# A crossed running product in a chunked RWKV inverse, and sixteen modulation units moved to the gated linear mixer

## The chip, the cores and the metric

One core of a Trainium2 chip runs the whole program. The metric is the device time in microseconds; the median of three runs of the kernel before is 2090.2 us (2086.09 to 2093.96).

## The reference, cut to what matters

The program computes two transformer blocks and a mixture of experts on 512 tokens of width 1024. Two parts of it matter here. The RWKV mixer of the first block is a recurrence over tokens with 8 heads of 64:

```python
def step(S, inp):
    r_t, w_t, k_t, v_t, a_t, b_t = inp
    sa = jnp.einsum("bhij,bhj->bhi", S, a_t)
    S = S * w_t[:, :, None, :] + sa[..., None] * b_t[:, :, None, :] + v_t[..., None] * k_t[:, :, None, :]
    return S, jnp.einsum("bhij,bhj->bhi", S, r_t)
```

The second block's gated linear mixer (`gla_scan`) has 4 heads with keys of 64 and values of 128. The second block's norms are scaled and shifted by a modulation: six vectors of 1024 that come from a conditioning vector c through `silu(c) @ w_mod + b_mod`. The kernel keeps them as 48 columns `mod` of 128 partitions (8 columns for each vector). The first 16 columns (shift and scale of the first norm) are needed before the mixers of the second block, the other 32 only after them.

## The kernel before, in words

Everything is written out by hand on five engines with semaphores. A tensor that TensorE makes goes through one of eight PSUM banks: `open_` waits until the bank is free, `close` says that it is full, `filled` and `emptied` are the waits on the two sides, and each engine runs its instructions in the order of its own program. All matrix products have line 383, all transposes 387, ScalarE's activations 1119, VectorE's two-tensor operations 1482 and 1488.

**The weight ring.** SyncE streams 1 MB units of weights through a ring of two slots. It issues the load of unit u when the count `weights_used` has reached u, that is when unit u-1 has begun: its first product (modulation) or its first split (GpSimd, for the large projections) increments the count. The order of the units is fixed: 14 of the first projection, 24 of the modulation, 4 of the first output projection, 33 of the feed-forward, 18 of the second input projection, 22 of the branches.

**A modulation unit** (`modulation(i)`) is a 1024 x 256 piece of w_mod. TensorE makes the two column products of the unit before it (from `mod_rows`, which ScalarE has evacuated with `mod_row`), then eight products of 128 x 32 with 256 columns, four concurrent column groups, into bank 7. The columns gather in the other half of bank 7. Units 0 to 7 lie between the heads of the SSD mixer, units 8 to 23 in Inverse, one in each of the levels 1 to 4 of each pair.

**Inverse.** For each pair of heads m = 0 to 3, each chunk of 64 tokens needs the inverse of a unit triangular 64 x 64 matrix, built up by doubling. There are eight such matrices on each half of the partitions (2 heads e, 4 tiles t; i is the chunk inside a tile of 128 tokens and so the half of the partitions). `gram` makes the 64 x 64 products of two tensors for both e, both i and all t: `abT`, `ab`, `akT`, `rbT`, `rkT`. Then five levels: U = LV x X (LV is `r_AT` masked to the level's blocks, X the running product `r_X` in the transposed form), ScalarE evacuates U into `r_U`; ZU and XU from U with `r_Z` and `r_X`; VectorE adds them to Z and X, each head's half by itself. `blocks` makes one such product: eight 64 x 64 products (16 instructions, since a float32 product is two) on the two diagonal quadrants, row half i to column half i. In between, `prepare(m + 1, lv)` makes the decays and normed keys of the next pair on TensorE, ScalarE and VectorE, for m < 3. Level 1 also has `wv`, level 5 the gram `rkT`. After the levels come `awa`, `aww`, `gt` (diagonal quadrants), `hh` (off-diagonal quadrants, twice as many products), `ry_r` and `ry_w`; VectorE's `begin_pair` makes the next pair's tensors, and `masked_gram` multiplies a gram by a mask while it is evacuated.

**The gated linear mixer.** Its attention inside tiles of 128 is made of eight levels. In each, TensorE makes `attn` of four heads (16 products, 32 instructions) and then `row_sums` of one squared tile for the q and k norms; VectorE merges the four results by a mask (`merge_level`), makes the level's log decays (`level_logs`) and, after ScalarE's two exponentials, two products for each m that make the next `attn` possible (`level_ready`). ScalarE's program for a level is: exponential m = 0, exponential m = 1, square.

Of the kernel before, what the change touches and what calls it, by code (L numbers as in the profile page):

```python
# [28 lines left out]
W_MOD_UNIT = 14  # L29
CH = 64  # L30
# [41 lines left out]
def build(nc, units, fixed, x, skew, out):  # L72
    ctx = ExitStack()
    with ctx:
# [181 lines left out]
        mod_rows = proj(ZZ + 4)[:, 0:256]  # L256
# [122 lines left out]
        def _(pe):  # L379
# [58 lines left out]
            def modulation(i):  # L438

                if i:  # L440
                    emptied(pe, "mod_rows", i - 1)
                    if i == 1:
                        pe.wait_ge(sem("sel_ready"), 1)
                    for j in range(2):
                        c = MOD_COLS + 2 * (i - 1) + j
                        last = mm(PSB[7][:, c:c + 1], mod_rows[:, j * P:(j + 1) * P], sel4[:, :])
                    if i == N_MOD:
                        last.then_inc(sem("mod_ready"), 1)
                        return
                u = W_MOD_UNIT + i  # L450
                pe.wait_ge(sem(f"weights{u % RING}_loaded"), 16 * (u // RING + 1))
                w = ring[:, u % RING, :].rearrange("p (k c) -> p k c", k=KT)
                o = open_("mod_rows", i, 7)
# [7 lines left out]
                close(last, "mod_rows", i)  # L461

# [83 lines left out]
            for h in range(8):  # L546
                m, e = h // 2, h % 2
                modulation(h)
# [24 lines left out]
            def gram(what, m, banks, l, r):  # L573
# [10 lines left out]
            def blocks(what, m, e, b, l, r):  # L584

                o = open_((what, m), e, b)
                for t in range(NT):
                    for i in range(2):
                        q = rows_of(i)
                        last = mm(c8(o)[q, t, :], c8(half(l, e))[q, t, :], c8(half(r, e))[q, t, :])  # L590
                close(last, (what, m), e)

            for m in range(4):
# [13 lines left out]
                gram("ab", m, (0, 1), ew(e_AT), ew(e_BH))  # L607
                gram("akT", m, (2, 4), ew(e_KH), ew(e_AT))
                gram("rbT", m, (5, 6), ew(e_BH), proj(RR + m))

                for lv in range(1, 6):
                    for e in range(2):
# [5 lines left out]
                        blocks(f"U{lv}", m, e, 3 * e, r_LV, r_X)  # L618
# [39 lines left out]
                o = open_("gt", m, 2)  # L658
                for t in range(NT):
                    for e in range(2):  # L660
                        for i in range(2):
                            q = rows_of(i)
                            last = mm(c8(o)[q, 4 * e + t, :], c8(r_AWA)[q, 4 * e + t, :], tm(t_BP)[q, t, rows_of(e)])
                close(last, "gt", m)
                emptied(pe, "aww", m)
                o = open_("hh", m, 5)
                for t in range(NT):
                    for e in range(2):
                        for step in range(2):
                            for i in range(2):  # L670
                                q, b = rows_of(i), 4 * e + t
                                l, r = ((tm(t_BP)[q, t, rows_of(e)], c8(r_AWW)[q, b, :]),
                                        (tm(t_KP)[q, t, rows_of(e)], tm(t_V)[q, t, rows_of(e)]))[step]
                                last = mm(c8(o)[rows_of(1 - i), b, :], l, r, step == 0, step == 1)
# [21 lines left out]
            modulation(N_MOD)  # L696
# [156 lines left out]
            sum_qk = open_("sum_qk", 0, 7)  # L853
            for lv in range(8):
# [13 lines left out]

# [1687 lines left out]
```

## Time and profile before

| | before |
|---|---|
| median of 3 runs | 2090.2 us |
| profiled execution, its own time | 2090.11 us |
| its span from the first to the last instruction | 2088.2 us |
| granted TensorE clock, mean | 0.91 |
| TensorE, VectorE, GpSimd, ScalarE busy | 1819.8, 1225.9, 677.4, 523.2 us |
| chain that ended last: TensorE, VectorE, ScalarE, DMA, issue | 70%, 17%, 5%, 4%, 3% |

Matrix products are pipelined, so a busy TensorE is not one at its peak; for small products the time of the weight loads (PEld) shows better how fast the queue moves. A row of a timeline begins with the start and the duration, and ends in brackets with the idle time before it and what ended that.

### The profile page before, as it was taken

To read this page: it belongs to the slowest core of one execution; us is meant where nothing else is said; L and a number is where in the kernel's file an instruction comes from. 1 tells how busy PE (TensorE), PEld (TensorE's weight loads), DVE (VectorE), ACT (ScalarE), POOL (GpSimd) and SP (SyncE) were. 2 spreads that over 40 slices of the span, in tenths; PEclk is the share of its full clock that TensorE was granted. 3 is DMA by queue.
4 is the path that set the end of the run, shared out by engine and by line. 5 is a ranking of instruction groups with operands and counts; after the bars stand their busy time and mean duration, and the time that the engine had idled before them with its cause. 6 is when DMAs were issued, how large, how long until landed. Compare 5 with 4: busy or idle time off the path is not lost.

```text
span 2088.2 us, 28577 instructions
## 1 busy us (share of the span) xinstructions
PE 1819.8 (87%) x11458; PEld 1397.5 (67%) x11458; DVE 1225.9 (59%) x1628; ACT 523.2 (25%) x775; POOL 677.4 (32%) x382
## 2 busy tenths in 40 slices
PE   6999667998878999999789999899889994877798
PEld 4887336777647777777467788777667763555565
DVE  6958255553358888888621495476444524555564
ACT  2121323441112010101221212220341124444453
POOL 2664000001234666666245471025234631000000
PEclk9999568998899999999899997589999996988899
DMA  4221222223114222222112130013211353766673
GB/s 191 97 85 63 83 77 83 84 84 103 37 45 143 89 97 83 100 80 100 40 64 99 61 101 21 1 41 106 71 61 61 101 201 126 277 265 271 266 308 149
DMA packets 34065, 230.46 MB, mean 110 GB/s; under 512 B 4132, under 2 KB 4388, under 8 KB 8232
## 3 DMA queue, kind: packets, MB, share of 16 engines
q1 hardware_dynamic: 30240, 214.48, 28.4%
q10 hardware_dynamic: 2136, 10.24, 1.3%
q0 software_dynamic: 1584, 4.21, 0.5%
q8 instruction: 82, 1.34, 0.3%
q14 instruction: 23, 0.19, 0.0%
HBM read 220.98 MB, written 9.50 MB: 110 GB/s over the span
## 4 chain that ended last, share of the span: by engine, by line
PE 70%; DVE 17%; ACT 5%; DMA 4%; issue 3%; POOL 0%; DVEq 0%; SPq 0%; ACTq 0%; POOLq 0%
PE psum L383 68%; DVE arena L1482 4%; DVE arena L1488 4%; PE psum L387 2%; DVE arena L1485 2%; DVE expert_lo L1482 2%; ACT arena L1119 2%; ACT L1119 1%; DMA weight_ring<-units 1%; ACT expert_hi L1119 1%; DVE tiny L1496 1%; DMA arena<-units 1%; DMA out<-arena 1%; DVE residual L1482 0%; ACT tiny L1119 0%
## 5 line engine op out<-in xcount | busy, mean ns | idle before, releaser
L1119 ACT ACTIVATE arena<-psum 128x512 f32<-128x512 f32 (+4 forms) x295 | 149.2, 521 | 916.2 <-PE psum L383 742.0
L383 PE MATMUL psum<-arena 64*64 64x64 f32 (+4 forms) x2828 | 272.0, 292 | 66.2 <-DVE arena L1482 52.2
L383 PEld LDWEIGHTS psum<-arena 64*64 64x64 f32 (+3 forms) x2828 | 196.5, 173 | 124.1 <-issue 73.9
L383 PE MATMUL psum<-normed_hi,w_in_hi 128*128 128x512 f32 x512 | 204.4, 399 | 14.3 <-DVE in_lo L1482 8.3
L383 PE MATMUL psum<-normed_hi,w_in_lo 128*128 128x512 f32 x512 | 203.3, 397 | 0.0
L1482 DVE TENSOR_TENSOR arena<-arena,psum 128x512 f32<-128x512 f32 (+2 forms) x200 | 112.1, 588 | 153.8 <-PE psum L383 105.5
L383 PE MATMUL psum<-in_lo,w_in_hi 128*128 128x512 f32 x512 | 201.7, 394 | 0.0
L1488 DVE SCALAR_TENSOR_TENSOR arena<-arena,fixed_data 128x512 f32<-128x512 f32 x134 | 188.9, 1410 | 13.5 <-DVE arena L1485 0.2
L2302 POOL TENSOR_TENSOR w_ff_lo<-weight_ring,w_ff_hi 128x1024 fp32r<-128x1024 f32 x66 | 166.6, 2524 | 5.5
L2302 POOL TENSOR_TENSOR w_in_lo<-weight_ring,w_in_hi 128x1024 fp32r<-128x1024 f32 x64 | 163.0, 2547 | 5.3
L383 PE MATMUL psum<-arena,fixed_data 128*128 128x512 f32 (+10 forms) x424 | 130.6, 473 | 36.6 <-DVE arena L1482 18.1
L1482 DVE TENSOR_TENSOR arena<-arena 128x512 f32<-128x512 f32 (+3 forms) x202 | 144.9, 729 | 15.5 <-PE psum L383 7.3
L383 PE MATMUL psum<-normed_hi,w_ff_hi 128*128 128x512 f32 x352 | 139.2, 396 | 11.6 <-DVE in_ff_lo L1482 11.6
L383 PE MATMUL psum<-in_ff_lo,w_ff_hi 128*128 128x512 f32 x352 | 140.7, 400 | 0.0
L383 PE MATMUL psum<-normed_hi,w_ff_lo 128*128 128x512 f32 x352 | 140.6, 400 | 0.0
L2295 POOL TENSOR_SCALAR w_in_hi<-weight_ring 128x1024 fp32r<-128x1024 f32 x64 | 72.1, 1127 | 199.9 <-PE psum L383 189.0
L2295 POOL TENSOR_SCALAR w_br_hi<-weight_ring 128x1024 fp32r<-128x1024 f32 x44 | 46.5, 1057 | 276.2 <-PE psum L383 159.4
L2295 POOL TENSOR_SCALAR w_ff_hi<-weight_ring 128x1024 fp32r<-128x1024 f32 x66 | 73.9, 1120 | 174.8 <-PE psum L383 174.8
L1482 DVE TENSOR_TENSOR expert_lo<-arena,expert_hi 128x2048 fp32r<-128x2048 f32 x36 | 81.1, 2288 | 82.5 <-ACT expert_hi L1119 82.4
L2295 POOL TENSOR_SCALAR w_out_hi<-weight_ring 128x1024 fp32r<-128x1024 f32 x8 | 8.9, 1108 | 371.9 <-PE psum L383 370.3
L383 PEld LDWEIGHTS psum<-normed_hi,w_in_hi 128*128 128x128 f32 x512 | 96.8, 189 | 42.7 <-issue 15.4
L2347 POOL DMA_INDIRECT out<-arena x7 | 6.8, 978 | 340.8 <-DVE arena L1482 340.8
(225 smaller groups left out, 3674.0 us busy)
## 6 DMA issues: line engine op xcount, KB each, us to landing
weight_ring<-units SPq DMA_DIRECT2D x124, 1024.0 KB, 4.9
arena<-units SPq DMA_DIRECT2D x55, 1024.0 KB, 8.2
normed<-units SPq DMA_DIRECT2D x20, 1024.0 KB, 8.8
slots<-arena ACTq DMA_DIRECT2D x7, 516.0 KB, 5.1
arena<-slots SPq DMA_DIRECT2D x7, 516.0 KB, 3.4
fixed_data<-fixed ACTq DMA_DIRECT2D x1, 2944.0 KB, 12.0
arena<-x SPq DMA_DIRECT2D x4, 512.0 KB, 6.0
arena<-bias_rows ACTq DMA_DIRECT2D x2, 896.0 KB, 5.2
```

The source lines that it names most:

```text
L383: return nc.tensor.matmul(o, l, r, start=start, stop=stop)
L387: return nc.tensor.transpose(o, i, C("ident", k, 0, k))
L1119: return nc.scalar.activation(o, i, func, **kw)
L1482: return V.tensor_tensor(o, a, b, op)
L1485: return V.tensor_scalar(o, a, s1, s2, op0) if op1 is None else V.tensor_scalar(o, a, s1, s2, op0, op1)
L1488: return V.scalar_tensor_tensor(o, a, s1, b, op0, op1)
L1496: V.reciprocal(v_tmp, v_tmp).then_inc(sem("variance_inverted"), 1)
L2295: first = nc.gpsimd.tensor_scalar(hi, raw, 1.0, 1.0, ALU.mult, ALU.mult)
L2302: nc.gpsimd.tensor_tensor(lo, raw, hi.bitcast(F32), ALU.subtract).then_inc(sem("split_ready"), 1)
L2347: nc.gpsimd.indirect_dma_start(out[:, :], bass.IndirectOffsetOnAxis(ap=xb[b % 3][:, D + 4:D + 5].bitcast(I32), axis=0), xb[b % 3][:, 0:D], ...
```

## The change

It has two parts.

**Crossed product.** X is now kept on the other half of the partitions: the matrix of chunk i lies on half 1-i. `ab` is written crossed (`gram(..., crossed=True)`), and a second gram of the transposed kind, `abT_crossed`, is added for LV (`r_AT`); `abT` now only gives Z. U is made from half 1-i to half i, on the off-diagonal quadrants. ZU (half i to i) and XU (half i to 1-i) are written product by product in turn, two of each. `gt` and `hh` are interleaved in the same way. VectorE masks one more gram and makes one multiply less per pair.

**Moved units.** Modulation units 8 to 23 leave Inverse. They are used inside the gated linear mixer, two in each of the eight levels, between `attn` and `row_sums`, with rows in bank 6 and columns in bank 5 (`mod2`). Their rows go to `tiny`. ScalarE evacuates the two after each square. VectorE adds the bias to columns 0 to 15 where it did before, and to 16 to 47 after the last merge. The ring's order follows: the sixteen units come after the second input projection's, SyncE's loop is cut into four, and GpSimd skips 8 and then 16 units. The column products of unit 7 now stand at the end of the SSD mixer.

```diff
+N_MOD1 = 8
+W_MOD2_UNIT = 77
...
-            def modulation(i):
-                if i:
-                    emptied(pe, "mod_rows", i - 1)
...
+            def mod_rows_in(i):
+                u = W_MOD_UNIT + i if i < N_MOD1 else W_MOD2_UNIT + i - N_MOD1
                 pe.wait_ge(sem(f"weights{u % RING}_loaded"), 16 * (u // RING + 1))
...
+            def mod_columns(i, o):
+                emptied(pe, "mod_rows", i)
+                if i == 0:
+                    pe.wait_ge(sem("sel_ready"), 1)
+                for j in range(2):
+                    last = mm(o[:, 2 * i + j:2 * i + j + 1], mod_rows[i >= N_MOD1][:, j * P:(j + 1) * P], sel4[:, :])
+                return last
...
-                            last = mm(c8(o[e])[rows_of(i), t, :], l[rows_of(e), c], r[rows_of(e), c])
+                            last = mm(c8(o[e])[rows_of(1 - i if crossed else i), t, :], l[rows_of(e), c], r[rows_of(e), c])
...
+            def block(o, q, e, t, l, r):
+                return mm(c8(o)[rows_of(q[1]), t, :], c8(half(l, e))[rows_of(q[0]), t, :], c8(half(r, e))[rows_of(q[0]), t, :])
...
-                gram("ab", m, (0, 1), ew(e_AT), ew(e_BH))
-                gram("akT", m, (2, 4), ew(e_KH), ew(e_AT))
-                gram("rbT", m, (5, 6), ew(e_BH), proj(RR + m))
+                gram("abT_crossed", m, (0, 1), ew(e_BH), ew(e_AT), True)
+                gram("ab", m, (2, 3), ew(e_AT), ew(e_BH), True)
+                gram("akT", m, (4, 5), ew(e_KH), ew(e_AT))
+                gram("rbT", m, (6, 1), ew(e_BH), proj(RR + m))
...
-                        blocks(f"U{lv}", m, e, 3 * e, r_LV, r_X)
+                        for t in range(NT):
+                            for i in range(2):
+                                last = block(o, (1 - i, i), e, t, r_LV, r_X)
...
-                    if lv < 5:
-                        modulation(8 + 4 * m + lv - 1)
-                    else:
+                    if lv == 5:
                         gram("rkT", m, (2, 5), ew(e_KH), proj(RR + m))
...
-                        blocks(f"ZU{lv}", m, e, 3 * e + 1, r_U, r_Z)
-                            blocks(f"XU{lv}", m, e, 3 * e + 2, r_Z, r_U)
+                        for t in range(NT):
+                            for i in range(2):
+                                z = block(oz, (i, i), e, t, r_U, r_Z)
+                            if lv < 5:
+                                for i in range(2):
+                                    x = block(ox, (i, 1 - i), e, t, r_Z, r_U)
...
             sum_qk = open_("sum_qk", 0, 7)
+            mod2 = open_("mod2", 0, 5)
             for lv in range(8):
...
+                for i in (N_MOD1 + 2 * lv, N_MOD1 + 2 * lv + 1):
+                    if i > N_MOD1:
+                        mod_columns(i - 1, mod2)
+                    mod_rows_in(i)
                 pe.wait_ge(sem("sq_qk"), lv + 1)
                 last = row_sums(sum_qk, lv, sq_qk)
...
                 act.wait_ge(sem("sq_qk_used"), lv)
                 f(sq_qk, p2(DQ + lv), ACT.Square).then_inc(sem("sq_qk"), 1)
+                for i in range(2):
+                    mod_row(N_MOD1 + 2 * lv + i)
...
-                masked_gram("abT", m, r_AT, k_strict)
+                masked_gram("abT", m, r_Z, k_level[0])
+                masked_gram("abT_crossed", m, r_AT, k_strict)
...
-                link(tt(c8(r_Z), c8(r_AT), rep8(k_level[0]), ALU.mult))
+                link(tt(c8(r_Z), c8(r_Z), rep8(k_ident), ALU.add))
                 masked_gram("ab", m, r_X, k_level0t)
-                link(tt(c8(r_Z), c8(r_Z), rep8(k_ident), ALU.add))
...
+            filled(dve, "mod2")
+            tt(mod[:, 16:48], PSB[bank_of("mod2")][:, 16:48], S("b_mod", 16, 32), ALU.add).then_inc(freed("mod2"), 1)
...
+            stream(RING, W_MOD_UNIT + N_MOD1, 0)
+            stream(W_MOD_UNIT + N_MOD1, W_MOD2_UNIT, n_mod2)
+            stream(W_MOD2_UNIT, W_MOD2_UNIT + n_mod2, W_MOD_UNIT + N_MOD1 - W_MOD2_UNIT)
+            stream(W_MOD2_UNIT + n_mod2, W_EXP_UNIT, 0)
```

## Rows read from the trace of the kernel before

**Rows 1.** The head of the page: span and instructions.

```profile
span 2088.2 us, 28577 instructions
```

**Rows 2.** Table by stretches: us; PE, PEld, DVE, ACT, POOL busy; clock; DMA share; GB/s.

```profile
464.30:494.80 30.50, 26.45 (x596) 22.10 (x597) 11.64 (x29) 5.97 (x15) 0.00 (x0) 0.89 0.42 140
...
1275.50:1327.00 51.50, 50.04 (x313) 48.11 (x313) 42.64 (x84) 13.48 (x22) 0.00 (x0) 0.54 0.00 1
...
1338.00:1366.00 28.00, 27.29 (x94) 21.85 (x95) 1.19 (x6) 4.79 (x10) 0.00 (x0) 0.50 0.00 0
```

**Rows 3.** Timeline of pair 0, a level, weight loads: start us, us, instruction [idle before].

```profile
341.65 0.55 PEld L383 LDWEIGHTS psum<-arena,normed 64*64 64x64 f32 x16 [0.41 <-issue]
...
343.67 0.29 PEld L383 LDWEIGHTS psum<-arena,fixed_data 64*128 64x128 f32 x2
...
344.72 1.01 PEld L383 LDWEIGHTS psum<-arena 64*64 64x64 f32 x32 [0.76 <-issue]
...
346.33 0.59 PEld L383 LDWEIGHTS psum<-weight_ring,smalls 128*32 128x32 f32 x16
```

**Rows 4.** The chain that ended last, the ring's load there: start us, us, what.

```profile
347.12 5.03 DMA weight_ring<-units
```

**Rows 5.** Timeline of pair 1: gt and hh begin, what follows them, a gram.

```profile
406.36 0.92 PEld L383 LDWEIGHTS psum<-arena,normed 64*64 64x64 f32 x28 [0.71 <-DVE arena L1482]
...
409.17 0.20 PEld L383 LDWEIGHTS psum<-arena,fixed_data 128*64 128x64 f32 x4
...
416.28 0.56 PEld L383 LDWEIGHTS psum<-arena 64*64 64x64 f32 x32 [0.17 <-issue]
```

**Rows 6.** Timeline of pair 2, U1 to U5: TensorE's loads and ScalarE.

```profile
419.96 1.01 PEld L383 LDWEIGHTS psum<-arena 64*64 64x64 f32 x32 [1.65 <-DVE arena L1482]
...
422.56 0.60 ACT L1119 ACTIVATE arena<-psum 128x512 f32<-128x512 f32 x1 [1.02 <-PE psum L383]
...
424.41 1.32 ACT L1119 ACTIVATE arena<-arena,fixed_data 128x512 f32<-128x512 f32 x2
...
425.75 1.28 ACT L1119 ACT_TABLE_LOAD   x1
...
428.61 0.64 ACT L1119 ACTIVATE normed<-psum 128x256 f32<-128x256 f32 x2
...
444.54 1.48 PEld L383 LDWEIGHTS psum<-arena 64*64 64x64 f32 x64 [0.76 <-issue]
```

**Rows 7.** Timeline of pair 3, U1 to U5, all engines.

```profile
464.29 3.48 PEld L383 LDWEIGHTS psum<-arena 64*64 64x64 f32 x64 [1.64 <-DVE arena L1482]
...
476.57 0.55 PEld L383 LDWEIGHTS psum<-normed,arena 64*64 64x64 f32 x16
...
477.38 0.75 DVE L1482 TENSOR_TENSOR arena<-arena,psum 128x256 f32<-128x256 f32 x2 [0.15 <-PE psum L383]
...
490.59 0.54 PEld L383 LDWEIGHTS psum<-arena 64*64 64x64 f32 x16 [0.15 <-DVE arena L1482]
...
491.32 0.38 ACT L1119 ACTIVATE normed<-psum 128x256 f32<-128x256 f32 x1 [2.31 <-PE psum L383]
```

**Rows 8.** Timeline: a unit's rows at the low clock (480.80); the mixer's levels.

```profile
480.80 1.43 PE L383 MATMUL psum<-weight_ring,smalls 128*32 128x256 f32 x16 [1.39 <-DMA weight_ring<-units]
...
1275.52 3.89 PEld L383 LDWEIGHTS psum<-arena 64*128 64x128 f32 x32 [2.39 <-ACT arena L1119]
...
1282.33 4.74 PEld L383 LDWEIGHTS psum<-arena 64*128 64x128 f32 x32 [0.92 <-DVE arena L1482]
...
1308.16 4.83 PEld L383 LDWEIGHTS psum<-arena 64*128 64x128 f32 x32
...
1309.59 0.63 ACT L1119 ACTIVATE arena<-arena 128x512 f32<-128x512 f32 x1 [0.69 <-DVE arena L1482]
...
1313.94 3.25 DVE L1482 TENSOR_TENSOR arena<-arena 128x256 f32<-128x256 f32 x8
...
1321.86 4.83 PEld L383 LDWEIGHTS psum<-arena 64*128 64x128 f32 x32
```

More of the change, by code:

```diff
@@ L436, in project @@
                     t0 += 1
-            def modulation(i):
-                if i:
-                    emptied(pe, "mod_rows", i - 1)
[L442 to L450, printed above, removed]
+            def mod_rows_in(i):
+                u = W_MOD_UNIT + i if i < N_MOD1 else W_MOD2_UNIT + i - N_MOD1
                 pe.wait_ge(sem(f"weights{u % RING}_loaded"), 16 * (u // RING + 1))
                 w = ring[:, u % RING, :].rearrange("p (k c) -> p k c", k=KT)
-                o = open_("mod_rows", i, 7)
+                o = open_("mod_rows", i, 7 if i < N_MOD1 else 6)
                 for r in range(2):
@@ L547, in _ @@
                 m, e = h // 2, h % 2
-                modulation(h)
+                if h:
+                    mod_columns(h - 1, PSB[7][:, MOD_COLS:])
+                mod_rows_in(h)
                 if e == 0:
@@ L570, in _, with gram @@
                          lambda i: (sem("sq_ssd"), 2 * g + i + 1))
-            def gram(what, m, banks, l, r):
+            mod_columns(N_MOD1 - 1, PSB[7][:, MOD_COLS:]).then_inc(sem("mod_ready"), 1)
+            def gram(what, m, banks, l, r, crossed=False):
                 o = [open_((what, m), e, banks[e]) for e in range(2)]
@@ L657, in _ @@
                 emptied(pe, "awa", m)
-                o = open_("gt", m, 2)
+                emptied(pe, "aww", m)
+                og, oh_ = open_("gt", m, 2), open_("hh", m, 5)
                 for t in range(NT):
                     for e in range(2):
+                        b = 4 * e + t
                         for i in range(2):
                             q = rows_of(i)
[L663 to L668, printed above, removed]
+                            last = mm(c8(og)[q, b, :], c8(r_AWA)[q, b, :], tm(t_BP)[q, t, rows_of(e)])
+                        if b == 7:
+                            close(last, "gt", m)
                         for step in range(2):
                             for i in range(2):
-                                q, b = rows_of(i), 4 * e + t
+                                q = rows_of(i)
                                 l, r = ((tm(t_BP)[q, t, rows_of(e)], c8(r_AWW)[q, b, :]),
                                         (tm(t_KP)[q, t, rows_of(e)], tm(t_V)[q, t, rows_of(e)]))[step]
-                                last = mm(c8(o)[rows_of(1 - i), b, :], l, r, step == 0, step == 1)
+                                last = mm(c8(oh_)[rows_of(1 - i), b, :], l, r, step == 0, step == 1)
                 close(last, "hh", m)
@@ L1332, in _ @@
                 f(sq_qk, p2(DQ + lv), ACT.Square).then_inc(sem("sq_qk"), 1)
+                for i in range(2):
+                    mod_row(N_MOD1 + 2 * lv + i)
             for m in range(2):
@@ L1765, in _ @@
             dve.wait_ge(sem("mod_ready"), 1)
[L1766 to L1768 removed]
+            tt(mod[:, 0:16], PSB[7][:, MOD_COLS:MOD_COLS + 16], S("b_mod", 0, 16), ALU.add).then_inc(sem("mod_added"), 1)
             dve.wait_ge(sem("ids_ready"), 2)
@@ L2321, in _ @@
             split_units(w_in1, 14)
-            unit[0] += N_MOD
+            unit[0] += N_MOD1
             filled(pool, "ry_w", 3)
@@ L2332, in _ @@
             split_units(w_in2, 18)
+            unit[0] += N_MOD - N_MOD1
             pool.wait_ge(sem("gla_out_ready"), 4)
@@ L2360, in _, with stream @@
                 sp.dma_start(ring[:, u, :], units[u, :, :]).then_inc(sem(f"weights{u}_loaded"), 16)
-            whole = n_units // RING - 1
-            with sp.Fori(0, whole) as i:
-                for j in range(RING):
-                    sp.wait_ge(sem("weights_used"), RING * i + j + 2)
-                    sp.dma_start(ring[:, j, :], units[bass.ds(RING * i + RING + j, 1), :, :].rearrange("a p n -> (a p) n"))\
-                        .then_inc(sem(f"weights{j}_loaded"), 16)
-            for u in range(RING * (whole + 1), n_units):
-                sp.wait_ge(sem("weights_used"), u - RING + 2)
-                sp.dma_start(ring[:, u % RING, :], units[u, :, :]).then_inc(sem(f"weights{u % RING}_loaded"), 16)
+            def stream(first, end, skip):
+                pairs = (end - first) // RING
+                with sp.Fori(0, pairs) as i:
+                    for j in range(RING):
+                        sp.wait_ge(sem("weights_used"), RING * i + (first + j - RING + 2))
+                        sp.dma_start(ring[:, (first + j) % RING, :],
+                                     units[bass.ds(RING * i + (first + j + skip), 1), :, :].rearrange("a p n -> (a p) n"))\
+                            .then_inc(sem(f"weights{(first + j) % RING}_loaded"), 16)
+                for u in range(first + RING * pairs, end):
+                    sp.wait_ge(sem("weights_used"), u - RING + 2)
+                    sp.dma_start(ring[:, u % RING, :], units[u + skip, :, :]).then_inc(sem(f"weights{u % RING}_loaded"), 16)
+            n_mod2 = N_MOD - N_MOD1
+            stream(RING, W_MOD_UNIT + N_MOD1, 0)
+            stream(W_MOD_UNIT + N_MOD1, W_MOD2_UNIT, n_mod2)
+            stream(W_MOD2_UNIT, W_MOD2_UNIT + n_mod2, W_MOD_UNIT + N_MOD1 - W_MOD2_UNIT)
+            stream(W_MOD2_UNIT + n_mod2, W_EXP_UNIT, 0)
             def load(o, u, name):
```

32 lines of the change are left out of this document (16 added, 16 removed).

## The prediction

> **What bounds the kernel now.** The page comes first: its engines' shares say TensorE, but a share is a mean over stages, so the next view is the chain that ended last and then the table by stretches, for the two stages that the change touches. The profiled execution spans 2088.2 us [rows 1]. In the RWKV stage ("Inverse": four pairs of heads, each a loop of five levels) TensorE is busy for 26.45 of 30.50 us of the last pair, at 0.89 of the full clock (its levels are 1.2 and 2.4 GHz, so a mixture), while VectorE has 11.64 [rows 2]. In the level loop of the gated linear mixer it is busy for 50.04 of 51.50 us, at 0.54 of the full clock, beside 42.64 us of VectorE [rows 2]. The reader is to see that the place the modulation units go to has no idle TensorE to put them in.
>
> The timeline of one level of pair 0 shows what a level is made of [rows 3]. Weight loads show where the queue stands: ZU and XU begin at 341.65, the preparing product of the next pair at 343.67, U of the next level at 344.72, the row products of the modulation unit at 346.33. So ZU and XU take 2.02, prepare 1.05, U 1.08 (its loads 1.01 and a handover), the unit's two column products the other 0.53 before its rows, and the rows 0.59 plus 0.41 of issue, which stands as idle time in the row at 341.65 too: 5.7 in all.
>
> The last part is the weight ring. It has two slots, but the load of unit u is issued only when unit u-1 has begun. The unit begins at 346.33 [rows 3]; its successor's load is issued at 347.12, once the first row product is done, takes 5.03 us and lands at 352.15 [rows 4]. Two units can't begin less than 5.8 us apart. Inverse has one unit per level and hardly feels that. The new place has two per level, back to back.
>
> **Part 1, modulation out of Inverse.** Sixteen units of 0.53+0.59+0.41 = 1.53 us leave TensorE: 24.5 us, with 16 evacuations of 0.4 us on ScalarE and 16 loads on SP. Not all of it is gained, as the next limit is near.
>
> **Part 2, the quadrants.** A gram puts products on all four quadrants of 64x64: 32 instructions load in 0.56 us [rows 5]. U has two quadrants: 32 in 1.01 [rows 3]. U stays on two (the off-diagonal ones), and so does ZU of level 5; ZU and XU interleaved get four. 64 instructions go from 2.02 to about 2 x 0.56 = 1.1: 0.9 per level, 16 levels, 14 us of TensorE. gt and hh now run from 406.36 to 409.17, 2.8 us for 96 instructions [rows 5]; interleaved, the off-diagonal pair still has 64, so some 1.9 remain: 0.9 per pair. The extra gram costs TensorE 0.56 per pair beside a wait of VectorE. On VectorE the crossed mask (two halves, 0.75 as the pair of operations in [rows 7]) replaces a multiply about as long that was done while it waited for the ab gram; the new one isn't hidden, since crossed grams come after the transposes. So 0.75 per pair goes back on the path to U1. These two leave +0.15 per pair; bounds -0.9 to +0.9.
>
> In a gram each row half writes a bank of its own; in the new ZU and XU both row halves write both banks. No row here has four quadrants with shared banks, so the gram's 0.56 is the nearest row, and the 2.02 of now the other bound. The Trainium skill (TensorEngine Tiling (Array Packing), Restrictions and Gotchas) says that different row tiles can't access the same PSUM bank at the same time. That rule speaks against this part: by it the sum would come out as in rival C. The trace has nothing that agrees or disagrees.
>
> **Levels of pairs 0 to 2**, worked forward from U1 as time 0 with pair 2's durations. Before: U1 419.96, U5 444.54 [rows 6], so 24.6 us. After: wv's evacuation ends at 3.2, as now (422.56 + 0.60); the next pair's two activations (1.3) follow at once, no longer behind a unit's evacuation; then the table load (1.28) and the sigmoid and identity (1.6, from the load's end at 427.03 to U2's evacuation at 428.61) end at 7.3, where now it is 8.65 [rows 6]; with the first half evacuated (0.4) ZU2 begins at 7.7. ScalarE bounds this level. Products 1.1, prepare 1.05: U3 at 9.9, its evacuation waits for the next sigmoid, ZU3 at 11.1. VectorE then carries the next pair's two operations, the level mask and the four additions (1.45+0.7+1.5): U4 at 13.2, ZU4 14.4. The scan, the mask and the additions (1.5+0.7+1.5): U5 at 16.7. That is 7.9 less. Pairs 0 and 1 have the same queues; pair 0 starts at the low clock and keeps some of that. I take 7.5 and 6.9 for them. Together 22.3. From U5 on (masks of rkT, begin_pair) nothing changes.
>
> **Pair 3** has no preparing. U1 464.29 to U5 490.59 is 26.3 [rows 7], with the low clock at its start and three waits on the ring. Afterwards the chain of one level is: U to its evacuation 0.73 (490.59 to 491.32), evacuation 0.45, products to VectorE 0.81 (476.57 to 477.38), two additions 0.75 [rows 7]: 2.75, and with the mask in between 2.9. U1 to U2 is 5.0 if the low clock at its start stays (3.5 of loads for U1 and wv, 0.8 to VectorE, 0.75); then 3 x 2.9: 13.7, and I take 14.3 for the two halves' overlap. Saved 12; 9 if the clock stays low in it.
>
> Inverse in sum: 22.3 + 12 + 4 x 0.15 + 0.5 (the last unit's columns, now in SSD's idle tail) = **35 us less**. Bounds: 20 (no gain from the quadrants, 12, and pair 3 at the low clock, 3) to 43 (all the TensorE time, 24.5+14, and what the ring and the low clock take in pair 3).
>
> **Part 3, the mixer's levels.** Before, attn of level 5 begins at 1308.16 and that of level 7 at 1321.86: 6.85 per level, made of 5.05 of attn (4.83 of loads and a handover) and 1.8 of row sums; at the start of the loop, nearer the high clock, attn takes 3.9 [rows 8]. Now each level gets unit A and unit B between attn and the row sums, and on ScalarE their evacuations stand in the queue ahead of the exponentials of the next level. Those wait now for B's evacuation, though their inputs are long there; VectorE's products and attn wait for them. With B's start as 0 at the low clock: rows done 1.43 [rows 8] and evacuated (0.38, as U's half in [rows 7]) 1.85, one exponential 0.63, two of the eight VectorE operations (3.25) 0.9 with the handovers [rows 8]: attn at 3.45. Its two halves, 5.1, end at 8.6; columns of B 0.93, twice the 0.5 of the high clock less a little; A at 9.5. B's load begins once A's first product is done: 6.1 more, and B is at **15.6**. At the high clock 3.15 + 3.9 + 0.55 + 5.85 = 13.45. VectorE's work (merge and logs) falls into the ring's wait and costs nothing.
>
> Sum: attn 0 to attn 1 was 6.8 (1275.5 to 1282.33, [rows 2, 8]); now A0 at 1279.6, B0 at 1285.5, attn 1 at 1288.6: +6.3. Attn 1 to attn 7 was 39.5 (1282.33 to 1321.86, [rows 8]); now six periods, of which I take one at 13.45 and five at 15.6, since the loop falls to the low clock even when 97% busy and now idles for 5 us in each period: 91.5, so +52. After attn 7, VectorE went on 5.9 later; now attn 5.1, columns 0.9, 6.1, B 1.35, sums 1.8, columns 0.9 and the new additions of mod 0.4: 16.6, so +10.7. Together **69 us more**; bounds 55 (all at the high clock: 6.3 + 41 + 7.5) and 78 (loads of 5.8 instead of 5.0, low clock). Sixteen units would be 24.5 to 36 us of TensorE even without any wait, about what Inverse gets back; the rest is the ring and the queue order.
>
> Elsewhere: the loop of SP is cut in four, same waits, same bytes; POOL skips eight and sixteen units with the same ring parity, its first w_out and w_br units are still there early: 0. mod's second part is used from the routing on, much later: 0.
>
> **Sum:** 2090.1 (the profiled execution, 0.1 below the median of 2090.2) - 35 + 69 = **2124**.
>
> **Rivals.** A: the work of part 3 is hidden: the ring's wait doesn't come, for instance because the load of B is there early. Then a level at the high clock is attn 3.9, columns and rows 0.55 + 1.0, evacuation wait 0.5, columns 0.5, then 3.15 from B: 9.6 instead of 6.85, some 22 us over the stage; were the 28 us of [rows 2] behind the loop (clock 0.50) also at the high clock, 14 came back: 2090 - 35 + 22 - 14 = **2063**, faster. It decides from the point where A to B is under about 3 us. Against it: SP's wait counts units begun, and [rows 3, 4] have 5.8 from a start to the successor's landing. Chance 0.04. B: the pair of units warms the clock for the stage: +55, and 14 back later: 2090 - 35 + 41 = **2096**, the same. Against: 5 us idle in 13. Chance 0.05. C: two banks, not four quadrants, made the gram fast; ZU/XU stay at 2.0: each early level is up to 0.9 longer where TensorE decides and always in pair 3, gt/hh nothing: 12 us less gain, **2136**. For it: only the grams' layout is in the trace. Chance 0.15. D: with less to do TensorE drops to the low clock all through Inverse; its 64x64 products double (U 1.8, ZU/XU 2.2, prepare 2): levels of 6, as long as now; Inverse gains nothing: **2159**. Against: the last pair, the emptiest, ran at 0.89 [rows 2], with dips only. Chance 0.06. My forecast: 0.70.
>
> **Numbers.** The forecast's own spread is 2108 to 2138 (clock in the levels, gain of 30 to 40). The range 2102 to 2142 leaves out A, D, most of B. A measurement of this kernel can tell about 0.5%, 10.5 us, from no change: faster 0.04, same 0.06, slower 0.90.
>
> **What would show it.** In the changed profile: U1 to U5 near 17 us in pairs 0 to 2 and 14 in pair 3; 64 ZU/XU instructions in 1.1 us; attn starts 13 to 16 us apart with waits on the weight ring in the middle of each level and ScalarE's exponentials behind the second evacuation; clock near 0.5 there. Wrong if attn starts are under 10 us apart, or if U1 to U5 stays over 20.

## The result, and the profile after

The changed kernel has a median of **2122.8 us** (four runs, 2120.58 to 2123.45) against 2090.2 before: 1.0157 times as long, 95% interval 1.0138 to 1.0175. Inverse gained about 38 us, the gated linear mixer lost about 70.

The head of the page of the changed kernel, the row of the granted clock in its 40 slices, and its chain by line:

```profile
span 2121.0 us, 28855 instructions
...
PE 1819.0 (86%) x11586; PEld 1390.2 (66%) x11586; DVE 1225.4 (58%) x1633; ACT 522.2 (25%) x775; POOL 677.6 (32%) x382
...
PEclk9999558997999999998999975579999996998899
...
PE psum L385 68%; DVE arena L1500 4%; DVE arena L1506 3%; ACT arena L1135 2%; PE psum L389 2%; DMA weight_ring<-units 2%; DVE arena L1503 2%; DVE expert_lo L1500 2%; ACT L1135 2%; ACT expert_hi L1135 1%; DMA arena<-units 1%; DVE tiny L1514 1%; DMA out<-arena 1%; ACT tiny L1135 1%; DMA normed<-units 0%
```

The engines' sums tell nothing here. TensorE is busy for 1819.0 us, before for 1819.8, though the program is 33 us longer: what it saved in one stage it spent again in another, and what was added to the end is time in which it stands idle. Only landmarks show where. The first product of RWKV's output projection that waits last starts at 518.39 (before 555.00), the mixer's first `attn` at 1239.20 (before 1275.52 [rows 8]), its first large products behind the loop at 1372.16 (before 1338.35). So 36.3 us are ahead when the mixer starts and 33.8 behind when it ends. Inverse itself starts 1.8 us later than before (`last_decay` at 323.39 against 321.62), from the stage ahead of it; it takes 195.0 us instead of 233.4.

**Inverse.** The timeline of pair 0 in the changed kernel, U1 to U3, to be read beside [rows 3]:

```profile
333.36 2.10 PEld L385 LDWEIGHTS psum<-arena 64*64 64x64 f32 x64 [2.29 <-DVE arena L1500]
...
335.33 0.14 PEld L385 LDWEIGHTS psum<-normed,arena 64*64 64x64 f32 x2
...
336.46 0.29 PEld L385 LDWEIGHTS psum<-arena,fixed_data 64*128 64x128 f32 x2
...
337.51 1.01 PEld L385 LDWEIGHTS psum<-arena 64*64 64x64 f32 x32 [0.76 <-DVE arena L1500]
...
340.62 0.14 PEld L385 LDWEIGHTS psum<-arena,normed 64*64 64x64 f32 x2 [2.09 <-ACT normed L1135]
...
341.71 0.29 PEld L385 LDWEIGHTS psum<-arena,fixed_data 64*128 64x128 f32 x2
342.76 1.01 PEld L385 LDWEIGHTS psum<-arena 64*64 64x64 f32 x32 [0.76 <-DVE arena L1500]
```

ZU and XU (64 instructions) begin at 335.33 and the preparing product behind them at 336.46: 1.13 us, where it was 2.02. U on its two quadrants still takes 1.01. U2 to U3 is 5.25 us, because ScalarE and not TensorE decides in that level: ZU and XU of level 2 wait 2.09 us for its evacuation of U2 (340.62). From U1 at 333.36 to U5 at 349.32 it is 16.0.

**The mixer.** One level of its loop, at the low clock: B lands, its rows, the row sums, ScalarE, the next `attn`:

```profile
1264.10 0.20 PEld L385 LDWEIGHTS psum<-weight_ring,smalls 128*32 128x32 f32 x8 [3.60 <-DMA weight_ring<-units]
...
1265.96 1.78 PEld L385 LDWEIGHTS psum<-fixed_data,arena 128*128 128x128 f32 x8 [0.81 <-issue]
1266.10 0.38 ACT L1135 ACTIVATE tiny<-psum 128x256 f32<-128x256 f32 x1 [6.18 <-PE psum L385]
1266.38 1.14 ACT L1135 ACTIVATE arena<-arena 128x512 f32<-128x512 f32 x2
1267.04 3.27 DVE L1500 TENSOR_TENSOR arena<-arena 128x256 f32<-128x256 f32 x8 [8.33 <-ACT arena L1135]
...
1267.97 2.16 PEld L385 LDWEIGHTS psum<-arena 64*128 64x128 f32 x13 [0.23 <-DVE arena L1500]
```

The chain that ended last in the same loop says the same, with the ring's load in each of the eight levels:

```profile
1252.94 6.09 PE psum L385 x41
1259.20 4.86 DMA weight_ring<-units
1264.10 1.98 PE psum L385 x16
...
1266.48 0.53 ACT arena L1135
1267.04 0.44 DVE arena L1500
1267.50 0.44 DVE arena L1500
1267.98 7.08 PE psum L385 x41
1275.22 5.07 DMA weight_ring<-units
1280.33 1.98 PE psum L385 x16
```

A starts, its first product is done, SyncE issues the load of B, which takes about 5 us, and TensorE stands for 3.6 of them. From A to B it is 5.6 to 6.35 us in the eight levels. The table by stretches gives the price of that in clock (columns as in [rows 2]): the whole loop, one level at each clock, and the stretch behind the loop.

```profile
1239.20:1345.59 106.39, 79.81 (x556) 61.45 (x556) 40.70 (x80) 16.96 (x36) 0.00 (x0) 0.57 0.40 133
...
1267.98:1284.21 16.23, 12.69 (x81) 9.66 (x81) 5.94 (x13) 2.43 (x6) 0.00 (x0) 0.50 0.39 131
1284.21:1298.91 14.70, 10.60 (x80) 8.37 (x80) 5.84 (x13) 2.42 (x6) 0.00 (x0) 0.62 0.41 140
...
1372.00:1400.00 28.00, 27.48 (x100) 22.36 (x101) 1.44 (x7) 4.79 (x10) 0.00 (x0) 0.53 0.00 0
```

The loop from `attn` 0 to `attn` 7 takes 106.4 us instead of 46.3, with levels of 13.74, 15.04, 16.23, 14.70, 16.14, 14.63 and 15.91. TensorE is idle for a quarter of it and its clock is only 0.57 of full. Behind the loop it is at 0.53, before it was at 0.50 [rows 2]: nothing was warmed.

### The profile page after: what moved, and what is told of

The parts are those of the page before. It is cut to its first block, busy times and chain, and to the rows that moved or that the text cites. A ratio compares the mean times of both kernels' runs of the same rounds, so it can differ in the third digit from the quotient of the medians.

```text
span 2121.0 us, 28855 instructions
## 1 busy us (share of the span) xinstructions
PE 1819.0 (86%) x11586; PEld 1390.2 (66%) x11586; DVE 1225.4 (58%) x1633; ACT 522.2 (25%) x775; POOL 677.6 (32%) x382
## 3 DMA queue, kind: packets, MB, share of 16 engines
q10 hardware_dynamic: 2136, 10.24, 1.3%
## 4 chain that ended last, share of the span: by engine, by line
PE 70%; DVE 16%; ACT 6%; DMA 5%; issue 3%; POOL 0%; DVEq 0%; SPq 0%; ACTq 0%; POOLq 0%
PE psum L385 68%; DVE arena L1500 4%; DVE arena L1506 3%; ACT arena L1135 2%; PE psum L389 2%; DMA weight_ring<-units 2%; DVE arena L1503 2%; DVE expert_lo L1500 2%; ACT L1135 2%; ACT expert_hi L1135 1%; DMA arena<-units 1%; DVE tiny L1514 1%; DMA out<-arena 1%; ACT tiny L1135 1%; DMA normed<-units 0%
## 5 line engine op out<-in xcount | busy, mean ns | idle before, releaser
L1135 ACT ACTIVATE arena<-psum 128x512 f32<-128x512 f32 (+1 forms) x279 | 143.1, 528 | 894.8 <-PE psum L385 726.1
L385 PE MATMUL psum<-arena 64*64 64x64 f32 (+5 forms) x2956 | 272.3, 289 | 65.8 <-DVE arena L1500 51.9
L385 PE MATMUL psum<-normed_hi,w_in_hi 128*128 128x512 f32 x512 | 204.6, 400 | 13.7 <-DVE in_lo L1500 7.7
L1506 DVE SCALAR_TENSOR_TENSOR arena<-arena,fixed_data 128x512 f32<-128x512 f32 x134 | 188.9, 1410 | 13.5 <-DVE arena L1503 0.2
L385 PE MATMUL psum<-arena,fixed_data 128*128 128x512 f32 (+10 forms) x424 | 131.1, 476 | 35.2 <-DVE arena L1500 16.8
L385 PEld LDWEIGHTS psum<-normed_hi,w_in_hi 128*128 128x128 f32 x512 | 97.1, 190 | 41.4 <-issue 15.4
```

The source lines that it names most:

```text
L385: return nc.tensor.matmul(o, l, r, start=start, stop=stop)
L1135: return nc.scalar.activation(o, i, func, **kw)
L1506: return V.scalar_tensor_tensor(o, a, s1, b, op0, op1)
```

## The experiments

Each ratio is to the kernel before on the same chip (medians of 2087.6, 2088.6 and 2090.2 us on the three chips used), so a difference between two times of different experiments is good to about 3 us. Diffs are against the changed kernel.

**1. Undo one part.** First the crossed products alone, with the units back in their levels:

```diff
-N_MOD1 = 8
+N_MOD1 = 24
...
+                    if lv < 5:
+                        unit_in(8 + 4 * m + lv - 1)
```

> The crossed product and the interleaving alone; all 24 modulation units stay where they were, one in each of levels 1 to 4 of a pair. Theory: the weight ring takes over as the limit of the levels. Two units can't begin less than 5.85 us apart, so U1 to U5 of a pair is 3.0 to the first unit, three spacings of 5.85, and 3.1 behind the last: 23.7 us against 25.4, 24.2, 24.6 and 26.3 before. Gain 5.6 in the levels and 0.6 from gt and hh: 2084 us (2080 to 2088). Rival: the quadrants give back the TensorE time they save, 14 us in the levels: 2075. Second rival: four quadrants are worth nothing beside the extra gram: 2090 or above.

Measured: 2094.0 us (2085.1 to 2097.7), 1.0016 [0.9998, 1.0034]. A miss: no gain, where 6 us were expected. Its timeline, units in pair 1 and in pair 3:

```profile
384.95 0.59 PEld L385 LDWEIGHTS psum<-weight_ring,smalls 128*32 128x32 f32 x16 [0.89 <-DMA weight_ring<-units]
...
390.51 0.59 PEld L385 LDWEIGHTS psum<-weight_ring,smalls 128*32 128x32 f32 x16 [0.81 <-DMA weight_ring<-units]
...
481.24 0.59 PEld L385 LDWEIGHTS psum<-weight_ring,smalls 128*32 128x32 f32 x16 [3.22 <-DMA weight_ring<-units]
```

These two units are 5.56 us apart and wait for their loads, as 11 of the sixteen do (11.3 us in all; before it were four, 2.5 us). From U1 to U5 the pairs take 24.1, 24.3, 23.0 and 24.4 us, in place of 25.35, 24.2, 24.6 and 26.3: TensorE is faster and waits for the ring instead. Inverse takes 233.9 us, as before (233.4). The levels gain 4.6 us. They are lost again: 2.7 us ahead of the first U1 and between the pairs, where the extra masked gram stands, and 2.5 between U5 of the last pair and the output projection, where TensorE stands once for 1.28 us (to 494.34) with nothing to wait for and goes on at the low clock.

Then the other half: units in the mixer, products as before on the diagonal quadrants.

```diff
-                                last = block(o, (1 - i, i), e, t, r_LV, r_X)
+                                last = block(o, (i, i), e, t, r_LV, r_X)
...
-                            if lv < 5:
-                                for i in range(2):
-                                    x = block(ox, (i, 1 - i), e, t, r_Z, r_U)
```

> The sixteen units moved to the mixer as in the change, with Inverse's products as before the change (no crossed product, no interleaving, one gram less). Theory: ZU and XU take 2.0 instead of 1.1 us, of which ScalarE's queue hides the part in levels 1 and 2 of pairs 0 to 2: 2.2 us more per pair there, 2 in pair 3, so about 8 us over the changed kernel: 2131 (2127 to 2135); the levels still shrink, since the units are gone. Rival: the quadrants carry all their TensorE time, 12 to 14 us: 2136. Second rival: they carry nothing: 2123.

Measured: 2128.0 (2126.1 to 2129.1), 1.0177 [1.0146, 1.0208], as expected to 3 us. In its timeline ZU and XU of level 2 begin at 339.78 and the preparing product at 341.80, the 2.02 us of before:

```profile
339.78 0.55 PEld L385 LDWEIGHTS psum<-arena,normed 64*64 64x64 f32 x16 [1.18 <-ACT normed L1135]
340.24 0.55 PEld L385 LDWEIGHTS psum<-normed,arena 64*64 64x64 f32 x16
...
341.80 0.29 PEld L385 LDWEIGHTS psum<-arena,fixed_data 64*128 64x128 f32 x2
```

With the landmarks `last_decay` and last wait of the output projection, Inverse takes:

| | units in Inverse | units in the mixer |
|---|---|---|
| products on the diagonal | 233.4 | 202.5 |
| crossed | 233.9 | 195.0 |

So moving the units is worth 31 us there and the crossing 7.5, but only once the units are gone. The parts don't add up; a sum by parts has to say in which order they are made. Each cell is one execution; Inverse of the changed kernel takes 193.9 to 195.4 us in the five profiled runs that leave it as it is, so 7.5 is good to 1.5 us.

**2. What the sixteen units cost in the mixer.** They are left out here, and mod's last 32 columns are the bias alone:

> The changed kernel without its sixteen later units at all: no loads, products, evacuations; their part of mod is the bias alone. Theory: what the units cost in the mixer is exactly what is missing from the changed kernel, 70 us, and Inverse keeps its 38: 2052 (2049 to 2056). Rival: part of the mixer's loss is not the units but the state in which the stage is entered (clock, DMA): then more than 2060.

```diff
-                for i in (N_MOD1 + 2 * lv, N_MOD1 + 2 * lv + 1):
-                    if i > N_MOD1:
-                        mod_columns(i - 1, mod2)
-                    mod_rows_in(i)
```

Measured: 2050.3 (2047.1 to 2053.7), 0.9816 [0.9799, 0.9834]: as expected. The units cost 2122.8 - 2050.3 = 72.5 us in the mixer (71 by the two ratios). Next the ring's part of it. Unit B uses the slot and the weights of A, so half of the later units' products use the weights of their neighbour, and nobody waits for a load between A and B:

```diff
-                        if r == 0 and j == 0:
+                        if r == 0 and j == 0 and (i < N_MOD1 or i % 2 == 0):
```

> The changed kernel with one load for the two units of a level: unit B multiplies the slot that A used, so eight loads and eight waits on the ring are gone, and the units' products of odd numbers are made from the wrong weights. TensorE's and ScalarE's instructions are the same. Theory: A to B falls from 5.7 to 6.4 us to what the columns and A's evacuation need, 2.6 to 3.4: 3.3 us less per level, 26 in all: 2097 (2090 to 2100), lower if the clock rises in the loop. Rival: the units' TensorE work and not the ring is what the mixer pays; then under 8 us are saved, 2115 or more.

Measured: 2093.6 (2091.7 to 2103.4), 1.0032 [1.0012, 1.0051], as expected. The profiled execution is one of the longer ones, 2100.8 us. Unit A and B in the timeline, and the loop with what follows it in the table by stretches:

```profile
1267.79 0.59 PEld L385 LDWEIGHTS psum<-weight_ring,smalls 128*32 128x32 f32 x16
...
1269.90 0.18 PEld L385 LDWEIGHTS psum<-weight_ring,smalls 128*32 128x32 f32 x8
```

```profile
1239.00:1343.00 104.00, 94.87 (x637) 72.94 (x634) 47.30 (x91) 19.99 (x41) 0.00 (x0) 0.53 0.24 82
```

A to B is 2.1 us here and in one more level, and 3.4 in the other six, instead of 5.6 to 6.35. That takes away 2122.8 - 2093.6 = 29 us (26 by the ratios; 22 between the two profiled executions). Some 43 to 45 stay: TensorE is busy for 91% of the stretch at 0.53. From `attn` 0 to `attn` 7 (1238.15 to 1324.45, 86.3 us) it is busy for 81.8 us, where it was 44.9 in the kernel before: 2.6 us for each of the fourteen units in between, which is their own work at a clock of 0.55. So even without the ring's wait the units cost more in the mixer than the 38 us that Inverse gained.

**3. Does ScalarE's order cost something?** The forecast put the exponentials behind B's evacuation on the path. Here they stand ahead of both:

```diff
-                for i in range(2):
-                    mod_row(N_MOD1 + 2 * lv + i)
...
+            for lv in range(0, 8):
...
+                if lv < 7:
+                    for m in range(2):
```

> The changed kernel with one order changed on ScalarE: in the mixer's levels the two exponentials of the next level come ahead of the evacuations of this level's two units. The forecast had attn of the next level wait for B's evacuation and the exponential (3.45 us behind B at the low clock, 3.15 at the high). Theory now, from the changed trace: at the low clock attn begins 3.9 us behind B, right when TensorE ends the row sums, so the queue order is covered and its removal changes nothing: 2122 (2120 to 2124). Rival, the forecast's words taken as they stand: the order costs about 1 us per level, 2114.

Measured: 2122.2 (2117.5 to 2124.0), 1.0142 [1.011, 1.0175]: nothing gained. Its timeline shows what stands beside it:

```profile
1265.80 0.20 PEld L385 LDWEIGHTS psum<-weight_ring,smalls 128*32 128x32 f32 x8 [3.59 <-DMA weight_ring<-units]
...
1267.66 1.78 PEld L385 LDWEIGHTS psum<-fixed_data,arena 128*128 128x128 f32 x8 [0.81 <-issue]
...
1269.46 2.79 PEld L385 LDWEIGHTS psum<-arena 64*128 64x128 f32 x19
```

`attn` follows the row sums without idle time, 3.66 us after B, where the changed kernel has 3.87. There `attn` does wait 0.23 us for the chain over ScalarE, but the row sums on TensorE end only that much earlier: the wait is real, and all but 0.2 us of it is covered.

**4. Spread the two units.** A between the halves of `attn`, B behind the row sums, ScalarE's exponentials between the two evacuations, all of the output kept:

```diff
+                    if m == 0:
+                        if lv:
+                            mod_columns(N_MOD1 + 2 * lv - 1, mod2)
+                        mod_rows_in(N_MOD1 + 2 * lv)
...
+                mod_columns(N_MOD1 + 2 * lv, mod2)
+                mod_rows_in(N_MOD1 + 2 * lv + 1)
```

> The changed kernel with the two units of a level spread: A between the attn of m = 0 and that of m = 1, B behind the row sums; ScalarE's exponentials of the next level between the two evacuations. All of the output is computed. Theory (the ring's spacing is the larger part of the mixer's price): between A's and B's starts lie 7.3 us of TensorE's work at the low clock, more than the ring's 6.1, so that wait goes; from B to the next A some 0.9 of waiting stays. A level falls from 15.2 to 13.2 or 13.6 us: 14 us less, 2108 (2100 to 2112). Rival: order doesn't matter, since TensorE's own work and the clock set the level: 2122. Lower bound: if the steady stream holds the high clock, a level is 11.7 and the time 2094.

Measured: 2106.4 (2105.1 to 2113.2), 1.0094 [1.0075, 1.0113]: as expected. Half of the ring's price is back, and the loop is bound by TensorE at the low clock: from 1240 to 1330 us it is busy for 89.0 of 90 us at a clock of 0.50. Its timeline has the units at 1262.28, 1269.82 and 1275.78, with waits of 0.30, none and 0.15 us:

```profile
1275.78 0.20 PEld L385 LDWEIGHTS psum<-weight_ring,smalls 128*32 128x32 f32 x8 [0.15 <-DMA weight_ring<-units]
```

**5. Units in the idle places of Inverse.** The crossed products stay, and the sixteen units go where the changed kernel's TensorE waits for VectorE or ScalarE: before U1, between U2 and ZU2, between U4 and ZU4, and behind `aww`.

```diff
+                unit_in(8 + 4 * m)
...
+                    if lv in (2, 4):
+                        unit_in(8 + 4 * m + lv // 2)
...
+                unit_in(8 + 4 * m + 3)
```

> The crossed products, and the sixteen units back in Inverse but put where the changed trace has TensorE waiting: before U1 (2.3 us idle there), between U2 and ZU2 (1.4 to 2.1), between U4 and ZU4 (nothing), and behind aww (1.1); the mixer as before the change. All of the output is computed. Theory: the units are 7 us and more apart, so the ring is never felt; of 1.53 us per unit 0.2, 0.3, 1.5 and 0.6 come on the path, 2.6 per pair, 10 in all, and 38 are gone as in the changed kernel: 2062 (2055 to 2068), faster than both. Rival: TensorE's work adds up wherever it stands: 38 less, 24.5 more, 2076. Second rival: four units per pair are bound by the ring as in the run with the quadrants alone: 2087.

Measured: 2072.6 (2066.1 to 2075.6), **0.9909 [0.9892, 0.9925]**: faster than both kernels, with the whole output. The size was missed by 10 us: Inverse takes 217.0 us, 22 more than without units, not 10. The rival that was put beside the forecast, 24.5 us of TensorE's work adding up wherever it stands (2076), comes nearer to the time. The timeline, the waits from 325 to 545 us, and a table of stretches show where:

```profile
340.59 0.96 PEld L385 LDWEIGHTS psum<-arena 64*64 64x64 f32 x17 [1.12 <-issue]
```

```profile
PE psum L385 <- issue: 5.2, 5, 1.5
```

```profile
334.77:340.00 5.23, 4.83 (x145) 3.82 (x145) 3.38 (x9) 3.70 (x6) 0.00 (x0) 1.00 0.62 204
340.00:345.00 5.00, 4.41 (x57) 3.01 (x61) 0.69 (x1) 2.59 (x6) 0.00 (x0) 0.59 0.15 21
345.00:350.00 5.00, 5.00 (x90) 3.38 (x84) 2.86 (x6) 1.07 (x2) 0.00 (x0) 0.50 0.49 195
```

In the middle of U2, with every input there, TensorE stands for about 1 us "for issue"; then the clock goes from 1.00 to 0.50 and the unit's rows run at the low one. Five such stalls, of 0.70 to 1.50 us, make 5.2 us; the clock falls within 2 us behind three of them (those that end at 340.59, 391.08 and 427.98) and stays at 1.00 behind the other two (413.90, 483.17). The same view of the changed kernel has no such row. From U1 to U5 the pairs take 6.6, 5.3, 2.8 and 2.1 us more than in the changed kernel, where the expectation has 1.8 for each. The last pair, which has no stall there, comes near that and stays under the 3.1 us that two units cost if they simply add up. So most of the miss lies in the three pairs with a stall and the low clock behind it, and the idle places do hide a part of the work.

The DMA's view of the same kernel has a candidate for the stalls. From 385 to 392 us it shows one packet of its instruction queue beside the ring's load:

```profile
q8 instruction: 1, 0.02, 0.8%
```

In windows of 0.1 us this packet (0.02 MB) is found at 388.7, and the ones ahead of the other stalls at 338.3, 411.7, 425.7 and 480.7: each time at the end of a ring load, and 2.2 to 2.5 us before the stall ends. The stall of 1.28 us in experiment 1 ends 2.4 us behind such a packet too (491.9). So TensorE may have waited for instructions that came late behind the ring's load. But packets at the end of a load without a stall exist as well (368.9, 443.8), and no run changed it: the cause is not shown.

**6. Is it the interleaving or the crossing?** X stays crossed, but ZU's products come first and XU's behind them, `gt` first and `hh` behind it, as before.

```diff
-                            if lv < 5:
-                                for i in range(2):
-                                    x = block(ox, (i, 1 - i), e, t, r_Z, r_U)
+                            for t in range(NT):
+                                for i in range(2):
+                                    x = block(ox, (i, 1 - i), e, t, r_Z, r_U)
```

> The changed kernel with the crossed product and its extra gram kept, but ZU and XU written one after the other and gt before hh, as before the change. Theory: the four quadrants pay by the order in which the products are written, not by the crossing. ZU and XU on two quadrants each take 2.0 us again instead of 1.13, gt and hh 2.8 instead of 1.9; what the units-only run showed (5 to 6 us over the changed kernel) comes back, and the mask of the extra gram (0.1 to 0.75 per pair) stays on top: 2130 (2127 to 2133). Rival: the queue overlaps the two products anyway, since ZU and XU are next to each other: 2123.

Measured: 2121.1 (2118.8 to 2124.0), 1.0149 [1.0123, 1.0176]. A miss: 2130 was expected, and it is as fast as the changed kernel. Its timeline, ZU and XU of level 2 and the preparing product behind them:

```profile
337.00 0.43 PEld L385 LDWEIGHTS psum<-arena,normed 64*64 64x64 f32 x12 [1.68 <-ACT normed L1136]
337.30 0.14 PEld L385 LDWEIGHTS psum<-normed,arena 64*64 64x64 f32 x2
...
338.50 0.18 PEld L385 LDWEIGHTS psum<-arena,fixed_data 64*128 64x128 f32 x1
```

64 instructions take 1.50 us: between 2.02 (diagonal) and 1.13 (in turn, two by two). The row behind the first shows where it is saved: XU's loads (`normed,arena`) start 0.30 us behind ZU's sixteen of that head (337.00 to 337.30), where with both on the same quadrants they start 0.46 behind (339.78 to 340.24, experiment 1). Order and number are the same in both, only the quadrants differ. So the crossing gives 0.5 us of the 0.9, and the written order 0.4. Inverse takes 197.1 us here, 2.1 more than with the order of the change (one execution each). The profiled run had started it 3.7 us earlier (319.65 against 323.39), from the stage ahead, and in the total such differences hide the 2 us.

## Why the prediction was right, and where not

**Sign, size and mechanism hold.** 2124 was forecast, 2122.8 came, and every one of the landmarks of "What would show it" is there: U1 to U5 of 16.0, 17.0 and 16.8 us and 13.65 in the last pair, 64 instructions in 1.13, `attn` starts 13.7 to 16.2 apart, waits of 2.7 to 3.6 us on the ring in the middle of each level, a clock of 0.57. In pair 2, for which the levels were worked forward, U3, U4 and U5 begin 10.2, 13.5 and 16.8 us behind U1, where 9.9, 13.2 and 16.7 were forecast. Term by term:

| term | forecast | measured |
|---|---|---|
| pairs 0 to 2, U1 to U5 | -22.3 | -9.4, -7.2, -7.8: -24.4 |
| pair 3, U1 to U5 | -12 | -12.6 |
| the rest of Inverse | -1.1 | -1.3 |
| Inverse | -35 | -38.4 |
| `attn` 0 to `attn` 1 | +6.3 | +6.9 |
| `attn` 1 to `attn` 7 | +52 | +53.1 |
| behind `attn` 7 | +10.7 | +10.1 |
| mixer | +69 | +70.1 |

In the sums Inverse misses by 3 us and the mixer by 1, to opposite sides; the stage ahead of Inverse adds 1.8 in this one execution, which was in no term. That the total comes within 1.2 us is luck to that extent. So is the row "the rest of Inverse", which adds a loss of 2.0 ahead of the pairs and between them to a gain of 3.3 behind the last, where the forecast had gains of 0.6 and 0.5.

**Part 2, the quadrants: right in the rate.** 1.13 us for 64 instructions against a forecast of 1.1 from the gram's row, so rival C is out. Here each row half writes both banks, and the rate is the gram's. By the rule of the Trainium skill (TensorEngine Tiling (Array Packing), Restrictions and Gotchas), by which different row tiles can't access the same PSUM bank at the same time, 2136 would have come; the trace doesn't agree with it as far as the rate goes. The trace of the kernel before already spoke to this, against what the prediction says: there U, ZU and XU have both row halves write one bank, and the sixteen instructions of each quadrant load in 1.01 us (0.063 each), while a gram's eight per quadrant load in 0.56 (0.07 each) [rows 3, 5]. `gt` and `hh` went from 2.8 to 2.05 us (355.87 to 357.92; forecast 1.9).

The split of Inverse's 35 us was off: rival C puts the quadrants at 12 of them and so the emptied levels at 23, and measured are 7.5 and 31. The two misses cancel.

**Part 2 rested on a wrong reason, though.** The step says that interleaving makes the four quadrants. Experiment 6 shows more than half of it from the crossing alone, since neighbours in the queue overlap where their quadrants differ. The forecast needed only the sum and didn't feel it.

**Three smaller things were missed in Inverse.** Pair 0 was said to keep some of its low clock, but its U1 loads in 2.10 instead of 3.30 us, 2.5 us better than the 6.9 taken. The gain of 0.15 per pair from `gt` and `hh` against the crossed mask didn't come: from U5 to the next U1 it is 20.2 us where it was 19.75. 0.4 of that is a wait that the interleaving adds and the step didn't name: the block for `gt` and `hh` in turn must begin with the wait for `aww`'s evacuation, which only `hh` needs. `gt` begins 6.55 us after U5 (349.32 to 355.87), and 6.14 in experiment 6 (346.91 to 353.05) and 6.15 before. "From U5 on nothing changes" failed for pair 3 too: from its U5 (457.33, before 490.59) to the output projection it is 61.1 us instead of 64.4. In the scan over chunks three of the five steps whose loads the timeline shows take 1.00, 1.00 and 1.44 us and not 1.78, where before only the first did: the clock falls later. That is 1.4 of the 3.3 us. The other 2 lie between U5 and the scan, 0.53 of it the last unit's columns; what the rest is stays open.

**Part 3, the mixer: right in size and path, one term too small.** The period was built from the ring (5.8; measured 5.6 to 6.35 from A to B) and from 3.45 us between B and `attn`, over ScalarE's queue. Measured is 3.87, and the chain goes the forecast way: rows 1.98, evacuation 0.38, exponential 0.53, two operations of 0.44, and `attn` waits last for VectorE. The term that was too small is B's rows. It took 1.43 from the row at 480.80 [rows 8] for the low clock, but the mean clock of that row is 0.70; in one level of the changed kernel the rows of A take 1.07 us at 1.00 (1258.40) and those of B 1.94 at 0.50 (1264.10). What the step left out is that TensorE's row sums end only 0.2 us earlier, so this path can't be shortened: experiment 3 took ScalarE's order away and gained nothing. "One period at 13.45, five at 15.6" is 15.2 on average; measured 15.4, but alternating between mean clocks of 0.61 and 0.50 instead of one and five.

**The rivals.** A (2063) needed A to B under 3 us, which never came in the changed kernel. The run with one load in experiment 2 brought it to 2.1 in two levels and 3.4 in six and gave 2093.6, not 2063: the rival's levels of 9.6 us were at the high clock, and these took 10.95 to 13.26 us, at 0.55. So it fails in its condition, and in its price as far as the experiment reaches. B (the clock warms up) is refuted by 0.57 in the loop and 0.53 behind it. D by a granted clock of 0.87 to 1.00 in Inverse's levels.

**The gain that isn't there.** 2050.3 without the units shows that the crossing with an emptied Inverse is good for 38 us. Where the change goes wrong is only the place of the units: 31 us (39 with the crossing in place) were gained in Inverse for 72.5 in the mixer, 26 to 29 of them waits on the ring and the rest TensorE time at about half the clock. In the idle places of Inverse they cost 22.

## What to carry to other kernels

Before moving work to another stage, read that stage's granted clock and idle time: here a stage that was full at 0.54 of the clock charged 1.94 us at its low clock for rows that take 1.07 at the high one, and the ring of two slots charged a full transfer, 5.6 us and more, for each pair of uses that follow back to back. Two limits that lie close together (here TensorE's levels of 5.7 us and the ring's 5.6) must be moved together: the crossing alone showed nothing, so test a change in all four combinations. And before you credit a schedule with a gain, try the old order with the new layout.

## What was not expected of the hardware

Small products on different quadrants overlap without being written in turn: 64 instructions of 64x64 took 2.02 us on the same two quadrants, 1.50 when blocks of sixteen go by turns to different pairs of quadrants, 1.13 when the products themselves do. Two row halves writing the same two banks cost nothing against the gram's rate. TensorE stood for 0.7 to 1.5 us with nothing to wait for in five places of one kernel, each 2.2 to 2.5 us behind a packet of the instruction queue at the end of a 1 MB load, and the clock fell behind three of them. And the clock in the mixer stayed near half when TensorE was 75% busy (0.57), 91% (0.53) and 99% (0.50, the spread units).
